# Attention beside attention on one core: the next head's logits ahead of a block of sums, and an exponential and a maximum ahead of the neighbouring step

## What is computed

```python
# differential attention: 4 heads, query blocks of 128, two maps m = 0, 1 of width 64
s = einsum("bhmqd,bhmkd->bhmqk", qb, kb) * scale
p = softmax(where(mask, s, -inf), axis=-1)
w = p[:, :, 0] - lam * p[:, :, 1]
out = einsum("bhqk,bhkd->bhqd", w, vb)        # then rms_norm over each head's 128 values
# stick-breaking attention: 8 heads of width 64
z = einsum("bhqd,bhkd->bhqk", qb, kb) * scale
log_1m = where(causal, log_sigmoid(-z), 0.0)
suffix = cumsum(log_1m, reverse=True) - log_1m
a = where(causal, exp(log_sigmoid(z) + suffix), 0.0)
out = einsum("bhqk,bhkd->bhqd", a, vb)
```

## Time and profile before

| what | value |
|---|---|
| time, median of 3 runs | 2633.48 us (2633.48 to 2644.3) |
| time of the profiled execution | 2638.0 us |
| its span, first to last instruction | 2636.2 us |
| TensorE busy, share of the span | 2515.8 us, 95% |
| mean granted TensorE clock | 0.977 of 2.4 GHz |
| attention stage, in that span | about 196 to 318 us |

### The profile page before, as it was taken

One profiled execution on the slowest core, in us unless ns is written; L12 is line 12 of the kernel. 1 busy time (PEld: TensorE's weight loads), 2 busy tenths in 40 slices (PEclk: granted clock), 3 DMA queues, 4 the chain that ended last, 5 costly groups with the idle time before them and its releaser, 6 DMA issues.

```text
span 2636.2 us, 32138 instructions
## 1 busy us (share of the span) xinstructions
PE 2515.8 (95%) x11714; PEld 2015.9 (76%) x11714; DVE 1393.3 (53%) x1935; ACT 663.8 (25%) x1075; POOL 1557.1 (59%) x1056
## 2 busy tenths in 40 slices
PE   7998999999989998899999998999999998999997
PEld 6885688888767774688967875867888786878875
DVE  6986652221389999868024336244356235525354
ACT  3106630110353444330022123133114312201002
POOL 3640267766789887467624756525763575666652
PEclk8998999999999999899999999999999999999998
DMA  9740023333222221122221222312331222223221
GB/s 299 231 136 1 33 80 96 96 96 96 96 80 80 95 80 64 52 97 96 80 80 48 96 81 64 96 34 65 96 96 49 80 80 80 81 95 96 96 73 43
DMA packets 230248, 231.40 MB, mean 88 GB/s; under 512 B 9115, under 2 KB 228092, under 8 KB 230012
## 3 DMA queue, kind: packets, MB, share of 16 engines
q1 hardware_dynamic: 227216, 229.33, 27.4%
q10 hardware_dynamic: 2924, 0.66, 0.1%
HBM read 227.87 MB, written 2.10 MB: 87 GB/s over the span
## 4 chain that ended last, share of the span: by engine, by line
PE 80%; DVE 10%; DVEq 4%; ACT 2%; issue 1%; POOL 1%; DMA 1%; POOLq 1%; ACTq 0%; SPq 0%
PE PS L1419 66%; DVE PS L2928 5%; PE PS L1268 3%; DVEq L2930 2%; PE PS L1996 1%; PE PS L2198 1%; PE PS L2215 1%; PE PS L956 1%; PE PS L2585 1%; PE PS L1987 1%; DMA spare<-in_ada_w 1%; DVE X L1058 0%; DVEq L2823 0%; PE PS L1640 0%; PE PS L863 0%
## 5 line engine op out<-in xcount | busy, mean ns | idle before, releaser
L1367 POOL TENSOR_TENSOR Wl<-raw,Wh 128x512 fp32r<-128x512 f32 (+2 forms) x768 | 1042.7, 1389 | 29.0 <-issue 1.4
L1361 POOL TENSOR_SCALAR Wh<-raw 128x2048 fp32r<-128x2048 f32 (+2 forms) x196 | 367.0, 1873 | 839.5 <-PE PS L1419 381.6
L1419 PE MATMUL PS<-Hh,Wh 128*128 128x512 f32 x1944 | 769.7, 396 | 60.1 <-POOL Wl L1367 22.4
L1419 PE MATMUL PS<-Hl,Wh 128*128 128x512 f32 x1944 | 764.0, 393 | 0.0
L1419 PE MATMUL PS<-Hh,Wl 128*128 128x512 f32 x1944 | 763.1, 393 | 0.0
L1419 PEld LDWEIGHTS PS<-Hh,Wh 128*128 128x128 f32 x1944 | 367.8, 189 | 150.8 <-issue 44.7
L1419 PEld LDWEIGHTS PS<-Hh,Wl 128*128 128x128 f32 x1944 | 367.9, 189 | 79.4 <-issue 0.7
L1419 PEld LDWEIGHTS PS<-Hl,Wh 128*128 128x128 f32 x1944 | 368.2, 189 | 78.4 <-issue 1.4
L1419 PE MATMUL PS<-Bh,Wh 128*128 128x512 f32 x688 | 271.7, 395 | 6.5 <-DVE Bl L3154 6.5
L1419 PE MATMUL PS<-Bl,Wh 128*128 128x512 f32 x688 | 270.0, 392 | 0.0
L1419 PE MATMUL PS<-Bh,Wl 128*128 128x512 f32 x688 | 269.8, 392 | 0.0
(11 more groups left out here) (486 smaller groups left out, 2980.8 us busy)
## 6 DMA issues: line engine op xcount, KB each, us to landing
raw<-in_w_in SPq DMA_DIRECT2D x44, 1024.0 KB, 5.6
raw<-in_w_ff SPq DMA_DIRECT2D x32, 1024.0 KB, 5.4
raw<-in_conv_w_in SPq DMA_DIRECT2D x24, 1024.0 KB, 5.1
raw<-in_ret_w_in SPq DMA_DIRECT2D x24, 1024.0 KB, 5.1
spare<-in_ada_w SPq DMA_DIRECT2D x20, 1024.0 KB, 8.1
raw<-in_w_up SPq DMA_DIRECT2D x20, 1024.0 KB, 5.4
raw<-in_w_out SPq DMA_DIRECT2D x8, 1024.0 KB, 5.1
raw<-in_conv_w_out SPq DMA_DIRECT2D x8, 1024.0 KB, 5.1
```

Of the source, the lines that this page charges most:

```text
L1361: pool.tensor_scalar(st.Wh[0:rows, slot, k, 0:g.width], st.raw_slot(slot)[0:rows, k, 0:g.width], 1.0, 1.0, ALU.mult, ALU.mult)
L1367: ins = pool.tensor_tensor(st.Wl[0:rows, slot, k, 0:g.width], st.raw_slot(slot)[0:rows, k, 0:g.width], st.Wh[0:rows, slot, k, 0:g.width].b ...
L1419: mm = pe.matmul(out, lhs, rhs, start=(k == parts[0][0] and n == 0), stop=(k == parts[-1][0] and n == 2))
```

## The change

Three lists are reordered; no instruction is added, removed or altered, and no semaphore wait is.

```diff
         pe.wait_ge(opened, 1)
         scores(0)
+        later_logits(0)
         for h in range(SH):
-            later_logits(h)
             first_logits(h)
...
             later_sums(h)
             turn(2 * h + 1)
+            if h + 1 < SH:
+                later_logits(h + 1)
             first_sums(h)
...
             first_softplus(h)
+            later_attend(h)
             if h and h % 2 == 0:
                 head_rstd(h // 2 - 1)
...
             if 2 * h + 2 < last:
                 exps(2 * h + 2)
-            later_attend(h)
             copy_wt(2 * h + 1)
             first_attend(h)
...
             weights(2 * h + 1)
+            first_max(h)
             if 2 * h + 2 < last:
                 maxima(2 * h + 2)
-            first_max(h)
-            if 2 * h + 2 < last:
                 weights(2 * h + 2)
```

## The result

The changed kernel takes 2656.97 us (median of 8 executions, 2655.44 to 2665.0), the kernel before 2639.1 us (8, 2633.48 to 2647.7). The ratio is 1.0071, 95% interval 1.0057 to 1.0086: slower by 0.7%. The forecast was 2645.6 us and a range up to 2655.0; the measured time lies 2 us above that range.

A forecast was written before the change was run, and what follows sets the result against it. TensorE, busy for 95% of the span, was taken as the bound. Waits of +8.7 us and two clock falls of +3.4 gave +12.1 us, from the median 2633.5 to 2645.6 us; range 2636 to 2655.

The forecast's parts named there:

- The walk through the queues: Stage's engine lists followed instruction by instruction: alternating turns of 17.0 and 13.63 us, +8.7 us in all without the clock.
- The rival that the waits are covered: In the stage, ScalarE runs ahead or rstd is signalled early, TensorE loses its old wait: -3 us, 2631; chance 0.15.
- the one that nothing happens: Rival: spare time of ScalarE and VectorE absorbs the stage's reordering, no change; counted within the 0.15 for covered waits.
- two falls are the likeliest: +3.4: TensorE's clock halves for some 3.4 us behind two of three 2.2 us idle times, 1.7 us lost each.
- with all of them doubled, +18.9 (2652): Rival: clock falls behind all three stage idle times, each lasting twice as long; part of the slower rival, chance 0.40.
- Six were followed by such a stretch: Of nine idle times of 1.7 to 2.9 us in the trace, six preceded a 1.2 GHz stretch: two in three.
- the likeliest case: Stage waits of +8.7 us plus two clock falls, +12.1 us in sum; its own range 2641 to 2649.
- The base: Whole kernel's time before, taken as the median 2633.5 us; the profiled execution, 2638.0, lay 4.5 above it.
- VectorE at no cost: `first_max` ahead of `maxima` on VectorE: cost nothing, cover about 1.5 us, the old 0.5 us wait goes.
- the cover that I named: On VectorE, first sums want `first_max` only behind the later logits, `exps` wants maxima behind `later_attend`: about 1.5 us.

The follow-up runs named there:

- filled: Changed kernel plus five matmuls of 256 columns that nobody reads, ahead of turn(2h+1) at h = 2, 4 and 6; 2644.99 us, ratio 1.0018.
- rstd_back: Changed kernel with `head_rstd` ahead of `later_attend` again on ScalarE; 2647.07 us, ratio 1.0024.
- act_only: Kernel before with ScalarE's edit alone, `later_attend` right behind `first_softplus`; 2646.5 us, ratio 1.0030.
- changed_again: The changed kernel run once more, unaltered, for a second profile and more executions; 2657.79 us, ratio 1.0069 against the kernel before.
- square_later: Changed kernel with `head_square` behind `later_softplus` on ScalarE; 2656.01 us, ratio 1.0057.
- gap_then_sums: Changed kernel with the later logits directly behind the first sums instead of ahead of them; 2646.45 us, ratio 1.0035.
- wide_behind: Changed kernel plus three matmuls of 128 rows between turn(2h+1) and the later logits at h = 2, 4 and 6; 2655.91 us, ratio 1.0057.
- pe_only: Kernel before with TensorE's edit alone, the next head's later logits ahead of the first sums; 2651.13 us, ratio 1.0040.
- filled_2: Changed kernel plus two matmuls of 256 columns ahead of turn(2h+1) at h = 2, 4 and 6; 2646.06 us, ratio 1.0027.
- sums_first: Changed kernel with later logits behind first sums, `head_rstd` ahead of `later_attend`, `head_square` behind `later_softplus`; 2634.22 us, ratio 0.9983 against the kernel before.
- dve_only: Kernel before with VectorE's edit alone, `first_max` ahead of `maxima`; 2644.37 us, ratio 1.0015.
- norm_later: sums_first with `head_norm` moved on VectorE from even h to behind `first_max` of the next odd h; 2635.63 us, ratio 0.9984 against the kernel before.

## Why the prediction was wrong

**The walk through the queues was right.** It gave an idle time of 2.2 us ahead of the transposes at h = 2, 4 and 6; measured 2.27 each time. It gave 1.2 us of waits at `weigh` and `scores`, measured 0.54 and 0.44, 1.0 in all; turns of 17.0 and 13.63 us without the clock, measured 17.17 and, in the filled kernel, 13.7; and +8.7 us in all, where the filled kernels, whose mean clock is not down, show +10 and +9. The reason for it, `head_rstd` behind `later_attend` and `turn` behind it, is shown by rstd_back and act_only, which take it out and put it in alone. The rival that the waits are covered is refuted, and so is the one that nothing happens.

**The step that failed is the clock term, "two falls are the likeliest: +3.4".** It had two factors and both were too small. The clock fell behind all three idle times, in both profiles, not behind two in three; and five of the six falls lasted two stretches, not one, so each of these cost up to 3.3 us (a turn of 16.97 against 13.63), not 1.7. In place of +3.4 the clock cost 10 us in the first profile's stage, and 10 to 15 us over all executions, by the slope or by the half. The rival "with all of them doubled, +18.9 (2652)" was the case that came, +18.7 by the ratio (0.0071 of 2640), and by the prediction's own chances it was only a part of 0.40. By the rule of the Trainium skill that the prediction cited (TensorE: Matmul & The Clock Gate, "HAM oscillation") nothing would have fallen; the two profiles of the changed kernel contradict it six times out of six, behind 2.27 us.

Two readings made the term too small. "Six were followed by such a stretch" is true of five of the nine idle times; the sixth, 2.86 us up to 2572.79 in the trace before, has a time at 1.2 GHz of 10.2 us, from 2572.0 to 2582.3. So a longer fall was on view, and the likeliest case left it out. And the three idle times were taken as three draws with two chances in three each, but they stand in turns that repeat, and in the first profile their falls are alike to a tenth of a microsecond in place and length.

The nine idle times also stood behind and ahead of other work. Here the later logits follow directly. Three groups of runs with the 2.27 us and the logits of 64 rows right behind them have mean clocks of 0.9716, 0.9713 and 0.9718 (changed, again, square_later); three in which other work comes first have 0.9748, 0.9742 and 0.9756 (act_only, gap_then_sums, wide_behind). Two of the second three are the changed kernel with one edit behind the idle time, and of changed_again and wide_behind, run side by side on one chip, all six mean clocks of the first lie under all ten of the second. So what follows the idle time has a part in the price; how much, mean clocks can't tell closely, since part of such a difference can lie behind the stage (in the stage itself, the profile of changed_again has 17.1 us at 1.2 GHz and that of wide_behind 6.8). How it acts was not tested, but the profiles have a pattern. In the profiles of the first three the clock fell behind nine of nine idle times, in those of the other three behind five of nine. The length goes with two things: when the fall begins after TensorE resumes, and what it works on then. With the logits next (wide_behind, pe_only and filled_2 counted in), the eight falls that began 0.4 to 1.0 us after lasted two stretches, and the four that began 1.4 to 2.4 us after lasted one. With the sums of 128 rows next (act_only, gap_then_sums, sums_first), all five falls began 0.2 to 0.9 us after and lasted one.

**The base was off as well.** The median before was taken from three executions, 2633.5; over eight it is 2639.1, and over the 34 executions of the next group of runs 2641.06. The prediction had seen that the profiled execution lay 4.5 us higher and went by the median all the same. From 2639.1 the rival's time would have been 2658.

**VectorE at no cost** held within the changed kernel, where TensorE comes to `weigh` late anyway. By itself that edit moved a wait of 0.5 us to a place of 0.74; the cover that I named was there only together with the other edits.

## What to carry to other kernels

Ahead of a reordering, list for every moved instruction who waits for what now stands behind it: here a norm of 1.4 us, left behind a wait by one moved line, stopped TensorE through a shared bank in a call that the diff doesn't touch. An idle time of the engine that bounds the kernel is to be priced with the clock behind it: the same 2.27 us cost 1 to 3 us more or 3 to 5 us more each, by what ran next, and 0.9 us of work without a purpose inside it took nearly all of that back. And what an order wins shows only where the wait's whole ring is opened: none of the three edits gained by itself, and the version that gained kept the short work of the others ahead of the long wait.

## What was not expected of the hardware

- TensorE's clock fell to 1.2 GHz behind idle times of 2.27 us although the engine worked without a pause behind them and, in square_later, for 13 us ahead of the first, and stayed there for 3.4 or 6.8 us of full work (windows above).
- With 1.35 us idle, falls were rare: one in three in the profile, and a mean clock of 0.9778 over twelve executions, no lower than the kernel before's 0.9771.
- The mean clock over the whole kernel lay between 0.9744 and 0.9780 for versions whose profile shows no fall in the turns (dve_only, norm_later, rstd_back, filled and the kernel before). The profiles have between 87 and 114 us at 1.2 GHz behind the stage, where the program is the same. That idle times in later stages meet the clock differently when everything ahead of them shifts is the likely reason, but it was not tested; it leaves some us of doubt in every difference of mean clocks above.
